# The SSD mixer of a fused four-layer kernel: dt chain after the eighth tile, cumulative sums broadcast in float32r, decays per pair of heads, group norms one group late

## The reference, cut to what matters

```python
def ssd_mixer(u, w_in, conv_w, conv_b, dt_bias, a_log, d_skip, norm_w, w_out):
    z, xbc, dt_raw = split(u @ w_in)                 # 2048, 3072 and 32 channels
    xbc = silu(causal_dwconv(xbc, conv_w, conv_b))   # 4 taps along the sequence
    xs, B, C = split(xbc)                            # xs: 32 heads of 64; B, C: 4 groups of 128 states
    dt = softplus(dt_raw + dt_bias); a = -exp(a_log)
    # 4 chunks of 128 positions; cs = cumsum(dt * a) inside a chunk
    y_diag = (C B^T * exp(cs_l - cs_s) * lower triangle) @ (xs * dt)
    states = B^T @ (xs * dt * exp(cs_last - cs))     # one per chunk, passed on with decay exp(cs_last)
    y_off  = (C @ entering state) * exp(cs)
    y = (y_diag + y_off + d_skip * xs) * silu(z)
    y = y * rsqrt(mean(y * y over each group of 512 channels) + eps) * norm_w
    return y @ w_out
```

## Time and profile before

| | before |
|---|---|
| median of 3 runs | 3242.62 us (3233.7 to 3242.68) |
| profiled execution, its own time | 3239.93 us |
| its span | 3237.8 us |
| PE busy | 3023.4 us, 93% |
| DVE, ACT, POOL busy | 1459.0, 1178.9, 1307.8 us |
| mean granted PE clock | 0.948 |
| share of PE in the chain that ended last | 84% |

### The profile page before, as it was taken

One profiled execution on the slowest core, in us unless ns is written; L12 is line 12 of the kernel. 1 busy time (PEld: TensorE's weight loads), 2 busy tenths in 40 slices (PEclk: granted clock), 3 DMA queues, 4 the chain that ended last, 5 costly groups with the idle time before them and its releaser, 6 DMA issues.

```text
span 3237.8 us, 33761 instructions
## 1 busy us (share of the span) xinstructions
PE 3023.4 (93%) x13476; PEld 2446.9 (76%) x13476; DVE 1459.0 (45%) x2111; ACT 1178.9 (36%) x1640; POOL 1307.8 (40%) x670
## 2 busy tenths in 40 slices
PE   6989979999999878999999998899999989999998
PEld 4866647888888766788888877797888867778886
DVE  5557761651352377354155056663422345433132
ACT  4422233542343455543244253003423334343232
POOL 4411105544444436544444546103444443054443
PEclk8989989999999989999999998579999999999999
DMA  2211103222223222233333322002323221022322
GB/s 111 95 37 40 39 14 104 92 97 94 96 97 98 72 69 67 90 98 98 98 98 98 97 79 72 1 1 65 105 93 103 86 85 64 14 91 91 104 93 83
DMA packets 74172, 253.11 MB, mean 78 GB/s; under 512 B 8353, under 2 KB 8353, under 8 KB 74017
## 3 DMA queue, kind: packets, MB, share of 16 engines
q1 hardware_dynamic: 73008, 247.55, 23.8%
q10 hardware_dynamic: 1008, 3.41, 0.3%
HBM read 248.83 MB, written 2.10 MB: 77 GB/s over the span
## 4 chain that ended last, share of the span: by engine, by line
PE 84%; DVE 8%; ACT 3%; issue 2%; DMA 1%; POOL 1%; DVEq 0%; POOLq 0%; ACTq 0%; SPq 0%
PE bank L366 22%; PE bank L368 22%; PE bank L367 22%; PE bank L1495 3%; PE bank L388 2%; PE bank L389 1%; PE bank L390 1%; PE bank L440 1%; PE bank L843 1%; PE bank L845 1%; PE bank L844 1%; DVE inv L446 1%; PE bank L856 1%; DVE lth L1340 1%; POOL wlo L2189 1%
## 5 line engine op out<-in xcount | busy, mean ns | idle before, releaser
L2189 POOL TENSOR_TENSOR wlo<-raw,whi 128x1024 fp32r<-128x1024 f32 (+2 forms) x497 | 1135.8, 2288 | 1842.4 <-ACT whi L311 1842.4
L311 ACT ACTIVATE whi<-raw 128x1024 fp32r<-128x1024 f32 (+2 forms) x497 | 501.3, 1009 | 1139.6 <-DMA raw<-in_f_up 487.2
L366 PE MATMUL bank<-h_hi,whi 128*128 128x512 f32 x2240 | 878.8, 392 | 24.5 <-ACT xbc L925 17.2
L367 PE MATMUL bank<-h_lo,whi 128*128 128x512 f32 x2240 | 873.7, 390 | 0.0
L368 PE MATMUL bank<-h_hi,wlo 128*128 128x512 f32 x2240 | 873.4, 390 | 0.0
L366 PEld LDWEIGHTS bank<-h_hi,whi 128*128 128x128 f32 x2240 | 422.3, 189 | 116.6 <-ACT xbc L925 17.7
L367 PEld LDWEIGHTS bank<-h_lo,whi 128*128 128x128 f32 x2240 | 422.1, 188 | 89.9 <-issue 2.2
L368 PEld LDWEIGHTS bank<-h_hi,wlo 128*128 128x128 f32 x2240 | 422.0, 188 | 87.8
L366 PE MATMUL bank<-act_hi,whi 128*128 128x512 f32 x864 | 336.2, 389 | 0.9 <-POOL wlo L2189 0.9
L368 PE MATMUL bank<-act_hi,wlo 128*128 128x512 f32 x864 | 336.1, 389 | 0.0
L367 PE MATMUL bank<-act_lo,whi 128*128 128x512 f32 x864 | 336.1, 389 | 0.0
(11 more groups left out here) (418 smaller groups left out, 3886.0 us busy)
## 6 DMA issues: line engine op xcount, KB each, us to landing
raw<-in_f_up SPq DMA_DIRECT2D x216, 512.0 KB, 3.5
raw<-in_f_dn SPq DMA_DIRECT2D x64, 512.0 KB, 3.4
raw<-in_ssd_xbc SPq DMA_DIRECT2D x24, 512.0 KB, 3.5
raw<-in_f_dn SPq DMA_DIRECT2D x32, 384.0 KB, 3.0
raw<-in_lru_in SPq DMA_DIRECT2D x20, 512.0 KB, 3.5
raw<-in_ev_in SPq DMA_DIRECT2D x20, 512.0 KB, 3.5
raw<-in_f_dn SPq DMA_DIRECT2D x32, 320.0 KB, 2.9
raw<-in_ssd_z SPq DMA_DIRECT2D x16, 512.0 KB, 3.5
```

The costliest lines, as they stand in the source:

```text
L311: act.activation(whi[:, s, 0:WIDTH[u]], raw[:, s, 0:WIDTH[u]], ACT.Copy).then_inc(hi_done, 1)
L366: pe.matmul(out, wh, hi, start=kt == 0, stop=False)
L367: pe.matmul(out, wh, lo, start=False, stop=False)
L2189: pool.tensor_tensor(wlo[:, s, 0:n], raw[:, s, 0:n], whi[:, s, 0:n].bitcast(F32), ALU.subtract)\
```

## The change: what it does

- **dt chain.** DVE and ACT run it before tile 8 instead of before tile 0, on 128 partitions. At its end the cumulative sum is cut into three float32r parts, which are stacked on partitions 0 to 95 of `cs3` (ACT and DVE, five more operations). The transposes of the decays (`natural`) follow tile 13.
- **x transposes.** PE does two after each of tiles 15 to 22, DVE copies two at the end of each of its iterations 16 to 23. The transposes still alternate between banks 4 and 5.
- **Decays.** Per head a 96-row float32r matmul spreads the sum, a second one adds the mask (-2^100 above the diagonal), and ACT takes the exponential straight from PSUM, in four pieces of 128 columns with the sum at the row as its bias. Per pair one more 96-row matmul gives the decay of the entering part; its exponential `ec` multiplies the entering product after PE instead of its input, so that the entering part is three 128-row matmuls per pair.
- **z.** Its tiles lie in banks 0 and 1 instead of 0 to 3. `gate` works in the bank.
- **Group norms** run inside the loop, one group late: squares on ACT, their sum on POOL, one pair of matmuls per group on PE, `Ln` and `Exp` on ACT instead of `Sqrt` and DVE's reciprocal, high parts on ACT, low parts on POOL. POOL also makes `xdd` and the selectors `selp`. ACT keeps C B and B.

```diff
+BANKS = {"ssd_dt": (3,), "ssd_z": (0, 1), "ssd_out": (4, 5, 0, 1), ...
...
+            def x_natural(i):
                 st.freed(pe, i)
                 if i == 0:
+                    pe.wait_ge(dt_dve, 7)
+                    pe.wait_ge(dt_act, 9)
                 w(pe, xdt_ok, i - 1)
                 for c in range(NC):
                     last = pe.transpose(bank[4 + i % 2][:, c * P:(c + 1) * P], xbc[:, i, c * P:(c + 1) * P], ident[:])
                 last.then_inc(tr_x, 1)
...
+            def decay_rows(i):
+                w(pe, p_S, 2 * i)
+                for e in range(2):
+                    h = 2 * i + e
+                    pe.matmul(bank[4 + e][:], sel3[0:96, h:h + 1].broadcast_to((96, P)), cs3[0:96, :], start=True, stop=False)
+                    pe.matmul(bank[4 + e][:].rearrange("p (c l) -> p c l", c=NC), ident_r[:],
+                              mask_r[:].unsqueeze(1).broadcast_to((P, NC, P)), start=False, stop=True).then_inc(p_cs, 1)
...
+                pe.matmul(bank[6][:], selp[0:96, i % 2, :], cs3[0:96, :], start=True, stop=True).then_inc(p_c2, 1)
+            def y_entering(i):
+                pe.wait_ge(g_ent, 3 * g + 3)
+                pe.wait_ge(p_xd, i + 1)
+                for c in range(1, NC):
+                    last = pe.matmul(chunk(bank[2], c), ent[:, c - 1, q * P:q * P + P], chunk(xbc[:, 20 + g, :], c), ...
+                last.then_inc(p_off, 1)
+            def y_diagonal(i):
+                w(pe, p_ev, i)
+                for e in range(2):
+                    pe.wait_ge(p_S, 2 * i + e + 1)
+                    for c in range(NC): ...            # bank[3], 64 columns of xdt each
...
+            for t in range(2, 24):
+                st.pe_tile(pe, t, rhs_h)
+                if t == 13:
+                    natural()
+                if 15 <= t <= 22:
+                    x_natural(2 * t - 30)
+                    x_natural(2 * t - 29)
+            c_b(0); b_natural(0, 0); z_blocks(2); states(0, 0); states(0, 1)
+            z_blocks(2); decay_rows(0); states(0, 2); z_blocks(4)
+            for i in range(NX):
+                y_entering(i)
+                if q == 1 and g: squares(g - 1, i + 1)
+                if q == 2 and g + 1 < SSD_G: b_natural(g + 1, i + 1)
+                if q == 3 and g + 1 < SSD_G: states(g + 1, 0); states(g + 1, 1, i + 1)
+                z_blocks(4)
+                y_diagonal(i)
+                if i + 1 < NX: decay_rows(i + 1)
+                if q == 2 and g + 1 < SSD_G: c_b(g + 1)
+                if q == 3 and g + 1 < SSD_G: states(g + 1, 2)
+                z_blocks(4)
...
             for t in range(24):                        # ACT
+                if t == 8: dt_chain()
+                if t == 16:
+                    act.wait_ge(tr_dt, 2)
+                    act.activation(etot[:]..., bank[5][:, 0:P], ACT.Exp).then_inc(dt_act, 1)   # dt_act reaches 9
                 act.wait_ge(s_u, t + 1)
                 act.activation(st.bank(t)[:], ctap[:, t % 2, :], ACT.Identity, ...).then_inc(s_tap, 1)
                 st.split_ahead(t)
                 if t: silu(t - 1)
...
             for t in range(24):                        # DVE
+                if t == 8: dt_chain()
...
                 st.tile_ready(dve, t)
                 ...                                    # ctap and three taps, as before
+                if 16 <= t:
+                    x_natural(2 * t - 32)              # waits tr_x, increments xdt_ok
+                    x_natural(2 * t - 31)
...
+            for i in range(NX):                        # DVE
+                dve.wait_ge(p_off, i + 1)
+                dve.wait_ge(p_ec, i + 1)
+                dve.tensor_tensor(y, y, ec[:, P:T], ALU.mult).then_inc(p_om, 1)
+                dve.wait_ge(p_om, i + 1)
+                dve.scalar_tensor_tensor(out=xbc[:, i, :], in0=xbc[:, i, :], scalar=col("ssd_d", i), in1=bank[2][:], ...).then_inc(p_xd, 1)
+                if i: y_sum(i - 1)
+                for e in range(2):
+                    dve.wait_ge(p_E, 2 * i + e + 1)
+                    dve.tensor_tensor(t1[:, e, :], bank[4 + e][:], xbc[:, 16 + g, :], ALU.mult).then_inc(p_S, 1)
+                if i: gate(i - 1)
+                if q in (1, 2) and g: normed(4 * g + 2 * q - 6); normed(4 * g + 2 * q - 5)
+                if q == 3 and g + 1 < SSD_G: entering(g + 1)
...
+            def gate(i):                               # b is the bank of z tile i
+                dve.tensor_tensor(b, b, ipre[:], ALU.mult).then_inc(z_scaled, 1)
+                dve.wait_ge(z_tanh, i + 1)
+                dve.scalar_tensor_tensor(out=b, in0=zr[:], scalar=1.0, in1=b, ...).then_inc(z_gate, 1)
+                dve.wait_ge(z_gate, i + 1)
+                dve.wait_ge(p_ev, i + 1)
+                dve.scalar_tensor_tensor(out=xbc[:, i, :], in0=xbc[:, i, :], scalar=0.5, in1=b, ...).then_inc(zt.free(i), 1)
```

More of the change, by code:

```diff
@@ L847, in z_blocks, with c_b @@
                         last.then_inc(done, 1)
[L849 to L861, removed]
+            def c_b(g):
+                st.freed(pe, 20 + g)
+                w(pe, gn_n, 4 * (g - 1))
                 for c in range(NC):
@@ L879, in ssd_pe @@
[L879 to L899, removed]
@@ L927, in ssd_act @@
             for t in range(24):
+                if t == 8:
+                    dt_chain()
+                if t == 16:
+                    act.wait_ge(tr_dt, 2)
+                    act.activation(etot[:].rearrange("p a b -> p (a b)"), bank[5][:, 0:P], ACT.Exp).then_inc(dt_act, 1)
                 act.wait_ge(s_u, t + 1)
@@ L934, in ssd_act, with keep_b @@
             silu(23)
[L935 to L939 removed]
+            def keep_b(g):
+                act.wait_ge(g_bt, g + 1)
+                act.activation(bn[:].rearrange("p c l -> p (c l)"), bank[6][:], ACT.Copy).then_inc(g_bn, 1)
@@ new lines, in high @@
+            def high(j):
+                act.wait_ge(gn_n, j + 1)
+                act.activation(g_hi[:, j, :], xbc[:, j, :], ACT.Copy).then_inc(gn_hi, 1)
+            keep_b(0)
+            keep_cb(0)
+            exps(0)
+            for i in range(NX):
+                g, q = i // 4, i % 4
+                if i:
+                    z_tanh_of(i - 1)
+                if q == 1 and g:
+                    inverse(g - 1)
+                if q == 2 and g + 1 < SSD_G:
+                    keep_b(g + 1)
+                if q >= 2 and g:
+                    for k in (2 * q - 4, 2 * q - 3):
+                        high(4 * g - 4 + k)
+                if i + 1 < NX:
+                    exps(i + 1)
+                if q == 2 and g + 1 < SSD_G:
+                    keep_cb(g + 1)
+                if i:
+                    square(i - 1)
@@ L964, in ssd_act @@
+            z_tanh_of(NX - 1)
+            square(NX - 1)
+            inverse(SSD_G - 1)
+            for k in range(4):
+                high(12 + k)
             squares_behind(act, stage["ssd_out"], post0.stat, in_m, bank[6][:])
@@ L1103, in ssd_dve @@
+            y_sum(NX - 1)
+            gate(NX - 1)
+            for k in range(4):
+                normed(12 + k)
             so = stage["ssd_out"]
```

490 lines of the change are left out of this document (298 added, 192 removed).

## The result

The changed kernel is slower: 3313.36 us (median of 4 runs, 3311.39 to 3314.92) against 3238.16 us for the kernel before, run beside it (4 runs, 3233.41 to 3242.68). The ratio is 1.0232, with a 95% interval of 1.0211 to 1.0253. The profiled execution took 3312.69 us (span 3310.8), 72.8 us more than the 3239.93 us of before. The prediction was 3290, within 3240 to 3318. Its direction and the places of its waits are right, and its size is 23 us short.

A forecast was written before the change was run, and what follows sets the result against it. The prediction took PE's instruction order, with its holes, to set the time. Its terms, -17 + 14.8 + 1.5 + 53.5 + 9.7 + 32 - 44.7 = +49.8 us on 3239.9, gave 3290, range 3240 to 3318.

The forecast's parts named there:

- Step 1: dt chain moved to before tile 8: -17 us at tile 4, +14.8 for a hole before tile 11, +1.5 for `natural`.
- Step 2: x transposes among conv tiles: seven holes of 4.7 us with 2.0 restart, +53.5 in all; wait after tile 15, +9.7.
- Step 3: Tile 23 to last y: 245.1 us becomes 277.1, +32, with holes of 6.0 us and restarts in pairs 1 to 14.
- Step 4: Norms and first two output tiles, from the last y: 68.3 us becomes 23.6 without a hole, -44.7.
- B: All 24 holes occur but the clock stays up: 48 us less, 3242, no change; chance 0.10.
- C: Loop, pairs 1 to 14: DVE finishes the gate before PE asks for the bank; 112 us less, 3178; chance 0.14.
- D: Only the conv holes are absent because DVE copies in time: 47 us less, 3243; chance 0.05.
- E: Loop holes longer, ACT behind a split or table load, 2 us more a pair: 28 more, 3318; chance 0.05.

## Why the prediction was right, and where it was short

**Step 1** came out as forecast (12.53 for 12.7 before tile 11; 0.91 for 2.3 before tile 4). The chain has one thread, and in both places that were run the conv behind it waits; the run with the chain first shows that the move is worth little, as forecast.

**Step 2** had the mechanism and the wait right (4.65 for 4.7), shown by taking the wait away through order alone. The restart was mis-sized: 2.24 to 2.60 us here against the 2.0 taken, which is 0.5 us a turn in a turn of 13.59 against 13.1.

**Step 3** was right in sum (277.9 for 277.1) and nearly so in its parts: the loop 261.4 for 260.2, the first entering product 16.4 us behind tile 23 for 16.9, 14 holes of 4.2 to 5.9 us. The holes under 5.9 are in the turns where squares, B transposes or states fill the hole, which the forecast had allowed for. The last gate product took 0.69 us all 16 times, next to the 0.74 taken, and POOL was at work during each of them. That agrees with what the prediction said of POOL and DVE.

**Step 4** won what was forecast: 43.2 of 44.7 us, with no hole. A part of the missing 1.5 us is what the new address costs: the rows' inputs `g_hi` and `g_lo` lie in `big` too, and the 96 matmuls of two tiles (2 x 16 rows x 3) at 0.006 more are 0.6 us. The other part is the start: behind the wait of 2.73 us before the last y products the first four of these matmuls start 0.59, 0.43, 0.43 and 0.42 us apart instead of 0.23, about 1 us.

**The step that failed** is the last sentence of the sum: "Everything behind tile 1 of `ssd_out` is the same code and the same waits." Both are true, and the stretch, which the sum put at +0, is 18.2 us longer all the same, since the same code reads its input from another address. 19.5 us is what putting the address back is worth. Without it the forecast would have been 4 us off, so the step that failed is this term and not one of the four steps. This was to be seen in the diff, whose table of buffers has four new lines ahead of `big`, but no row of before shows what such a place costs.

**The rivals.** B (the clock stays up) is out: the granted clock was 0.76 in the conv stage and 0.85 in the loop (near 0.8 was forecast), and filling the waits gained time. C did not happen, but its place was right: the order alone decides, and 94 us hang on it. Its price of 112 was high, by the work in the holes that stays. D and E have nothing for them: the conv holes were there, and the loop's were no longer than 5.92 us.

## What to carry to other kernels

When a change reuses a buffer sooner or merges two stages, write down for each wait of the busiest engine which instruction frees the buffer and what stands ahead of it in that engine's program. Here two engines at under half load cost some 140 us by order alone; moving the freeing work and one exponential ahead of the next wait, and one buffer back, turned a loss of 2.3% into a gain of 2.8%. When buffers are added, look at the start address modulo 256 of every matmul operand behind them, keep the two operands of a matmul at the same one (64 and 64, or 0 and 0, were the fast pairs here), and put new buffers last.

## What the runs showed of the hardware

The pace of a float32r matmul of 512 columns at full clock depends on where its operands start. With the stationary operand 64 bytes above a multiple of 256, a streamed operand 64 above gives 0.227 us from start to start, 128 above about 0.229, and 192 above 0.233; with both at 0 it is 0.227. At 128 above one of the three lines of a block has a mean of 394 ns (L366), one of 392 (L368) and one of 388 (L367). With the roles exchanged (streamed 64 above, stationary 128 or 192) it is 0.233 and 0.232. Why is open.

Waits of 4.2 us and more in the mixer were each followed by a stretch at 1.2 GHz: a loss of 2.2 to 2.6 us in a conv turn, and of 1.3 to 2.9 (2.0 on average) in the loop. The wait of 0.91 us before tile 4 was followed by none: the matmuls behind it came every 0.23 us from the second on. In between it isn't settled by the length of the wait alone: behind 2.74 us the restart of the earlier trace rows was fast at once, and behind the 2.73 us before the last y products it was slow for the 16 small ones (2.32 us) and the first four output matmuls. What differed wasn't tried.
